# Making the pick diagonals on ScalarE in a four-step transformer block kernel

## The reference

```python
best_s, best_j = lax.top_k(cand_s.reshape(T, H, K * K), K)      # 8 heads x 16 picks a token
idx = jnp.take_along_axis(cand_i.reshape(T, H, K * K), best_j, axis=-1)
g = jax.nn.softmax(best_s, axis=-1)
u, v = expert_u[idx], expert_v[idx]
act = jax.nn.gelu(jnp.einsum('thkd,td->thk', u, xb), approximate=False)
return jnp.einsum('thk,thkd->td', g * act, v)
```

## Time and profile before

| | |
|---|---|
| median of three runs | 3788.93 us |
| the profiled execution itself | 3789.43 us |
| its span | 3787.6 us |
| TensorE matmul busy | 2901.6 us (77%) |
| VectorE busy | 2273.8 us (60%) |
| ScalarE busy | 682.6 us (18%) |
| GpSimd busy | 1153.4 us (30%) |
| moved by DMA | 1308.57 MB, of which gathers 1082.20 MB |

### The profile page before, as it was taken

How to read it: one execution, slowest core, us unless ns; L and a number is a source line. 1 busy time by engine, 2 the same in 40 slices (tenths; PEclk the granted TensorE clock), 3 DMA queues, 4 the chain that set the end, 5 groups by cost and what they waited for, 6 DMA issues and landing times. The chain is left out here.

```text
span 3787.6 us, 31946 instructions
## 1 busy us (share of the span) xinstructions
PE 2901.6 (77%) x11208; PEld 1477.7 (39%) x11208; DVE 2273.8 (60%) x5605; ACT 682.6 (18%) x1250; POOL 1153.4 (30%) x1044
## 2 busy tenths in 40 slices
PE   6689894689988876789988876788998845555555
PEld 3358661345644422345644422344563511111111
DVE  1230168776454888775454887776455688665665
ACT  1220011541111112531111112441111000000000
POOL 0000003443332333333333233332332325443442
PEclk9779996899998988899998977898998966777777
DMA  4125548899999999899999999889999969999998
GB/s 156 54 61 160 174 151 351 352 416 396 397 418 401 390 361 397 342 372 385 398 418 390 382 376 375 352 351 362 401 418 400 397 234 395 421 421 386 420 421 367
DMA packets 213745, 1308.57 MB, mean 345 GB/s; under 512 B 25537, under 2 KB 26321, under 8 KB 82001
## 3 DMA queue, kind: packets, MB, share of 16 engines
q0 software_dynamic: 149760, 1082.20, 70.5%
q1 hardware_dynamic: 63824, 224.33, 16.3%
HBM read 1292.80 MB, written 13.63 MB: 345 GB/s over the span
## 5 line engine op out<-in xcount | busy, mean ns | idle before, releaser
L608 POOL DMA_INDIRECT rowbuf<-in_peer_uv,idx x875 | 977.9, 1118 | 2214.3 <-PE acc L874 1475.2
L874 PE MATMUL acc<-rowbuf,diag 128*64 128x512 f32 x3500 | 1051.3, 714 | 443.4 <-DVE diag L1505 437.7
L1495 DVE CUSTOM_DVE_ANT_0 rowbuf<-rowbuf,xr 128x1024 f32<-128x1024 f32 x875 | 1049.9, 1222 | 402.3 <-DMA rowbuf<-in_peer_uv,idx 400.1
L874 PEld LDWEIGHTS acc<-rowbuf,diag 128*64 128x64 f32 x3500 | 254.9, 155 | 1051.3 <-DVE diag L1505 578.2
L1113 ACT ACTIVATE acts<-dots 128x2 f32<-128x2 f32 x512 | 104.0, 203 | 2337.3 <-DVE dots L1495 2245.0
L1505 DVE TENSOR_SCALAR diag<-consts,acts,gw 128x64 f32<-128x64 f32 x1024 | 285.3, 350 | 225.4 <-ACT acts L1113 101.0
L667 PE MATMUL bank<-xnT,W 128*128 128x256 f32 x1792 | 410.2, 385 | 0.0
L653 PE MATMUL bank<-W,xnT 128*128 128x512 f32 x832 | 377.9, 605 | 3.1 <-DVE xnT L1201 2.6
L667 PEld LDWEIGHTS bank<-xnT,W 128*128 128x128 f32 x1792 | 338.3, 192 | 91.9 <-issue 47.9
L667 PE MATMUL bank<-arena,W 128*128 128x256 f32 x1024 | 248.5, 402 | 38.3 <-DMA W<-in_w_blocks 35.9
L874 PE MATMUL acc<-kv,diag 128*64 128x512 f32 x468 | 176.0, 771 | 108.5 <-DVE diag L1505 98.4
(11 more groups left out here) (168 smaller groups left out, 2295.3 us busy)
## 6 DMA issues: line engine op xcount, KB each, us to landing
W<-in_w_blocks SPq DMA_DIRECT2D x360, 512.0 KB
rowbuf<-in_peer_uv,idx POOLq DMA_INDIRECT x875
xs<-in_x SPq DMA_DIRECT2D x16, 512.0 KB
xr<-x SPq DMA_DIRECT2D x32, 256.0 KB
out_y<-xs SPq DMA_DIRECT2D x8, 512.0 KB, 8.2
x<-arena SPq DMA_DIRECT2D x8, 512.0 KB
fin<-out_y POOLq DMA_DIRECT2D x8, 512.0 KB
out_y<-fin POOLq DMA_DIRECT2D x8, 512.0 KB, 16.6
```

The source lines that it names most:

```text
L608: pool.indirect_dma_start(rows[SLOT[g]], None, a["peer_uv"], bass.IndirectOffsetOnAxis(ap=idx[:, at // NB, at % NB:at % NB + 1], axis=0)). ...
L874: mm = pe.matmul(acc[HP * j:HP * (j + 1), h * HALF:(h + 1) * HALF], diag[:, c % DIAGS, j, :], v[:, D + h * HALF:D + (h + 1) * HALF], start ...
L1495: dve.tensor_tensor_reduce(out=u, in0=u, in1=xr[:, t, j, :], scale=1.0, scalar=0.0, op0=ALU.mult, op1=ALU.add, accum_out=dots[:, c % QS, j ...
```

## The change

`weigh` leaves VectorE. ScalarE makes the diagonals itself, directly behind each gelu, with two pairs of activations of the kind Copy: first `acts * gw` into a new 128x2 tile `scales`, then `ident2 * scales` into `diag`. It waits on its own semaphore after the gelu and after `scales`, and for `rows_added` of pick c-3. VectorE's `dot` gets a wait for the gelu four picks back, and before `rank` overwrites `gw` it waits for the diagonals of the step before.

```diff
@@ ScalarE
             def gelu(c):
                 act.wait_ge(dot_done, 2 * c + 2)
                 act.activation(acts[:, c % QS, :], dots[:, c % QS, :], ACT.Gelu).then_inc(gelu_done, 1)
+                act.wait_ge(gelu_done, c + 1)
+                at = 2 * (c % PAIRS)
+                for j in range(2):
+                    ins = act.activation(scales[:, c % QS, j:j + 1], acts[:, c % QS, j:j + 1], ACT.Copy,
+                                         scale=gw[:, c // PAIRS % NT, at + j:at + j + 1])
+                ins.then_inc(scaled, 1)
+                act.wait_ge(scaled, c + 1)
+                if c >= DIAGS:
+                    act.wait_ge(rows_added, c - DIAGS + 1)
+                for j in range(2):
+                    ins = act.activation(diag[:, c % DIAGS, j, :], ident2, ACT.Copy, scale=scales[:, c % QS, j:j + 1])
+                ins.then_inc(diag_ready, 1)
@@ VectorE, rank
+                if n > 1:
+                    dve.wait_ge(diag_ready, NT * PAIRS * (n - 2) + PAIRS * (t + 1))
                 dve.wait_ge(sm_exp, NT * (n - 1) + t + 1)
@@ VectorE, dot
                 t = c // PAIRS % NT
+                if c >= QS:
+                    dve.wait_ge(gelu_done, c - QS + 1)
@@ VectorE
-            def weigh(c):
-
-                dve.wait_ge(gelu_done, c + 1)
-                if c >= DIAGS:
-                    dve.wait_ge(rows_added, c - DIAGS + 1)
-                at = 2 * (c % PAIRS)
-                for j in range(2):
-                    ins = dve.tensor_scalar(diag[:, c % DIAGS, j, :], ident2, acts[:, c % QS, j:j + 1],
-                                            gw[:, c // PAIRS % NT, at + j:at + j + 1], ALU.mult, ALU.mult)
-                ins.then_inc(diag_ready, 1)
@@ VectorE, slot
-                weigh(c)
```

More of the change, by code:

```diff
@@ L341, in build @@
         acts = sb("acts", [P, QS, 2])
+        scales = sb("scales", [P, QS, 2])
         fin = sb("fin", [P, D])
@@ L467, in build @@
         gelu_done = sem("gelu_done")
+        scaled = sem("scaled")
         diag_ready = sem("diag_ready")
```

## The result

The changed kernel takes 3797.46 us, median of 17 runs (3789.31 to 3802.47), against 3786.24 us for the kernel before, also of 17 runs. The ratio is 1.0029 with a 95% interval of 1.0020 to 1.0038: 11 us slower. The forecast was 3788 us. The time is inside the range, but the forecast had the kernel level with before, by 1 us to the faster side, and it is slower beyond its interval.

A forecast was written before the change was run, and what follows sets the result against it. No engine was taken as the bound; DMA, TensorE, VectorE or a chain round all engines sets the pace by stage. -30 + 28 + 0.6 = -1 us on 3789.4 us gave 3788 us, range 3754 to 3820.

The forecast's parts named there:

- Where ScalarE is on the path: Attention units: picks ahead of the exponentials delay ScalarE's copy, 1.2 us a unit; 28 us together with the memory attention.
- Bound by stages: Whole kernel: no engine near its span; time moves only where DMA pauses, in routes and attentions, elsewhere gathers or matmuls.
- What leaves VectorE: Diagonals leave VectorE, 0.45 us a pick; 30 us gained, 22 of them in two route stretches, 0 elsewhere under cover.
- What ScalarE gets: Four activations and two own waits a pick: 1.34 us from gelu start to diagonals, what follows 1.1 us later.
- The other waits: Waits for `rows_added`, in `dot` and before `rank` cost 0 (`rows_added` at most 5 us); kernel's end +0.6 us.
- the slower one: Rival: ScalarE becomes the attentions' pace, 1.8 us a unit, routes give half; +32 us, 3821 us; chance 0.28.
- The faster one: Rival: rows go back sooner, so DMA fills its pauses in routes and attentions; -24 us, 3765 us; chance 0.35.
- The signs: Expected: VectorE busy 285 us less, route DMA share 0.98 or more, step 4 copies about 1.2 us further apart.
- The chances: Forecast 0.36, faster rival 0.35, slower rival 0.28, an own table load for each Copy 0.01.
- near cancellation: The forecast itself: gain and cost over the whole kernel nearly cancel, 3777 to 3800 us; chance 0.36.

The follow-up runs named there:

- ScalarE in the routes alone: Changed kernel, but ScalarE makes diagonals only for the 141 picks in the routes, VectorE all others; 3751.8 us, ratio 0.9935 to the kernel before.
- one slot later: Changed kernel with ScalarE's diagonals of a pick moved from behind its gelu to before the wait for the next dots; 3743.5 us, ratio 0.9912 to before.
- ScalarE only in the attentions: Changed kernel, but ScalarE makes diagonals only for the 69 picks in the attentions, VectorE all others; 3824.5 us, ratio 1.0127 to the kernel before.
- four diagonals: Changed kernel with four diagonal buffers in place of three; 3798.3 us, ratio 1.0055 to the kernel before.
- eight dots: Eight columns of dots and gelus in place of four; ratio to before 1.0060 in the changed kernel, 0.9909 with diagonals made one slot later.
- the kernel without diagonals: Changed kernel with diagonals set once at the start, TensorE waiting for the gelu alone, pick weights left out; 3722.6 us, ratio 0.9857 to before.

## Why the prediction was wrong

The kernel was forecast at 1 us under the one before, and it is 11 and 23 us over it, clear of noise. The step that failed is *Where ScalarE is on the path*: the cost there was put at 28 us and measured 48. The gain, put at 30 us, measured 25.

- **Bound by stages**: right. Pauses of DMA in routes and attentions were the places where the time moved; the tail is 0.4 us from before.
- **What leaves VectorE**, -30 us, nearly all in the routes: right in place, a little large in size. ScalarE in the routes alone gives -25 us, and it gives back 7.6 us ahead of the attentions. That one could read off 0 elsewhere from shares of 0.99 over 480 us was near enough by the times, though the profiles leave room for some us there.
- **What ScalarE gets**: right. 203, 287 and 340 ns, 1.34 us from the gelu's start to the diagonals (2442.17 to 2443.51), 1.13 us of delay for what follows. This is also the price by the figures of the Trainium skill (ScalarE: Activation LUTs, What ACT_TABLE_LOAD costs), some 280 and 333 ns, an estimate. The Trainium skill's rule that leaves multiplications to VectorE (ScalarE: Activation LUTs, Rules for kernel authors) goes by the time for an element, and the trace agrees that ScalarE takes longer for the work, 0.48 and 0.59 us against VectorE's 0.54. As a rule for the whole kernel it does not hold here: with the same four activations a pick one slot later the kernel is 0.9% faster than with VectorE.
- **Where ScalarE is on the path**, +25 us in the attentions and +3 us in the memory attention: this is the step that failed. It measured +48 us in all, of which the profile shows 34 us between the copies and 10 us ahead of them. Four terms of it were wrong. First, the share of the expensive units. I took about half to have a pick ahead of each exponential, from the number of picks a unit alone; it is 14 of the 18 that hold two exponentials. Their price, 1.8 us, was near the 2.0 us that they paid. Second, the price of a unit with a pick ahead of only one exponential. I took VectorE as the pace there and charged 0.5 us; they paid 1.7 us. The unit above shows ScalarE without a pause from its first gelu to the copy in just such a unit, since the load for the second gelu stands in the queue behind both exponentials; in these units a pick ahead of the copy costs its 1.1 us on either side of the exponentials. Third, TensorE's clock had no term. Its product behind the copy runs more often at the 1.2 GHz level, and that is most of the 8.2 us that lie behind the copy. Fourth, the half us of step 2 that the gathers were to cover did not show: 10.1 us over seven intervals is 1.4 us a unit. Steps 3 and 4 paid 1.8 and 1.9 us, at and over my upper bound. The memory attention was given 1 us a step. The stretch that holds it has 2.6 to 4.2 us with ScalarE only in the attentions, but three or four of the seven or eight picks there belong to the differential attention, so how far this price was too low stays open.
- **The other waits**: right. The one for `rows_added` was 52.5 us long in all, in 16 waits, so the add was not always done by then as I said, but without these waits nothing is gained (four diagonals). The wait of `dot` cost nothing that shows (eight dots). The end of the kernel is later by 0.56 us (1.34 against 0.78), as predicted.
- **The rivals**: the slower one was nearer in the mechanism, and its condition of about 1.7 us a unit was just met, with 36.3 us over 21 distances. But ScalarE is busy 59, 63 and 67 us of the 84, 99 and 114 us between the copies, not some 80%: it is the pace from the first gelu to the copy only. The routes gave more than the half that this rival left them, and the time stayed far from its 3821 us. The faster one's cause, rows that go back sooner, shows no gain by itself.
- **The signs**: VectorE's busy time fell by 254 us where I had 285, the route stretches reached a DMA share of 0.96 and not 0.98, and rank(4, 0) ends 5 us later (3117.2 against 3112.4 us), not earlier. The six distances of step 4 that hold two exponentials grew by 2.2 us on the mean, which was my own sign for the slower rival.
- **The chances**: 0.36 for a near cancellation and 0.28 for the slower case. Counting the units of the trace by where the gelus stand, and reading one of the other kind for ScalarE's idle time ahead of the copy, would have moved them. The two misses, 20 us of cost and 5 us of gain, push the same way; that the time is still in the range owes much to a range of 66 us.

## What to carry to other kernels

Work moved to an idle engine is priced by what stands behind it in that engine's queue, not by the engine's busy share. Put it in front of a wait that the engine has anyway: the same four activations cost 65 to 77 us behind the gelu and only 21 us ahead of the next wait for dots (3722.6 us without any, 3743.5 us so). Count such places in the trace one by one; an average number of picks a unit hid that 14 of 18 units were of the expensive kind. And where an edit helps in one stage and hurts in another, run it in each stage alone; the two effects here were 25 and 48 us behind a difference of 23.

## What the runs showed that was not expected

- The kernel to measure a delay against is the one without the work. Against the kernel before, a delay of 1.13 us behind each gelu seems to cost 36.3 us in the attentions and one of 0.62 us only 10.5 us. Against the kernel without diagonals it is 49 and 23 us.
- A longer wait of TensorE can be paid twice. Behind it the same product took 3.75 us at a granted clock of 0.50 where it had taken 2.02 us at 1.00, and such time is some 8 of the 36 us that the attentions lost.
- A table load takes 1.28 us and the activation behind it can start at once: 2443.52 to 2444.82 above, 1.30 us from start to start. The Trainium skill (ScalarE: Activation LUTs, What ACT_TABLE_LOAD costs) gives 2.66 us for a switch, with a drain of some 1.38 us. The trace differs: of the 217 loads of the changed kernel 126 take under 1.4 us from the end of the instruction ahead of them to the start of the one behind. The others can include waits and don't tell.
- The name in a wait's row is that of the next busy instruction. 88 us of waits at the dots belonged to another line's wait, as an experiment without the suspected wait and the same 18 waits in the trace of the kernel before both tell.
